# Weight units of half the size beside the row gathers of a two-block kernel

## The reference

```python
def peer(x, w_query, sub_keys, expert_down, expert_up):
    xt = x.reshape(T, D)
    qry = (xt @ w_query).reshape(T, H, 2, PEER_HALF_DIM)
    s = jnp.einsum('thpd,phnd->thpn', qry, sub_keys).astype(jnp.float32)
    ...
    gates = jax.nn.softmax(best_s, axis=-1).astype(x.dtype)
    ...
        u = expert_down[ib]
        act = jax.nn.gelu(jnp.einsum('td,thkd->thk', xb, u), approximate=False)
        vv = expert_up[ib]
        return jnp.einsum('thk,thkd->td', gb * act, vv)
```

## Time and profile before

| what | us |
|---|---|
| median of 3 runs | 3343.69 |
| lowest and highest of them | 3337.65, 3343.89 |
| the profiled execution | 3336.91 |
| its span in the trace | 3335.1 |
| PE busy in the span | 3110.8 (93%) |
| DMA: bytes moved, mean rate | 1206.86 MB, 362 GB/s |

### The profile page before, as it was taken

How to read it: one execution, slowest core, us unless ns; L and a number is a source line. 1 busy time by engine, 2 the same in 40 slices (tenths; PEclk the granted TensorE clock), 3 DMA queues, 4 the chain that set the end, 5 groups by cost and what they waited for, 6 DMA issues and landing times.

```text
span 3335.1 us, 24932 instructions
## 1 busy us (share of the span) xinstructions
PE 3110.8 (93%) x8525; PEld 1372.6 (41%) x8525; DVE 1087.6 (33%) x1830; ACT 570.1 (17%) x1356; POOL 641.3 (19%) x598
## 2 busy tenths in 40 slices
PE   8999998899999999998799989989799989999999
PEld 4444443444444444444244433434354533333344
DVE  1100014342334322335555544433432132222220
ACT  1110001111112110112224221221222111001010
POOL 1000002222224222223333332333300000000000
PEclk9999999999999999999999999999999989999999
DMA  9878887999989999999999999999967749999982
GB/s 351 305 273 294 307 299 292 414 370 360 397 343 396 421 417 407 402 411 405 420 408 419 418 419 419 419 419 417 416 220 267 258 194 422 422 422 422 422 310 76
DMA packets 266327, 1206.86 MB, mean 362 GB/s; under 512 B 14912, under 2 KB 17520, under 8 KB 162928
## 3 DMA queue, kind: packets, MB, share of 16 engines
q1 hardware_dynamic: 191872, 668.08, 52.0%
q0 software_dynamic: 74352, 537.48, 39.4%
HBM read 1203.41 MB, written 2.10 MB: 361 GB/s over the span
## 4 chain that ended last, share of the span: by engine, by line
PE 60%; DMA 30%; DVE 3%; issue 3%; ACT 1%; SPq 1%; DVEq 1%; POOL 0%; ACTq 0%; POOLq 0%
DMA W<-in_peer_expert_down,big 14%; PE bank L918 13%; PE bank L1469 11%; PE bank L987 8%; DMA W<-in_w_expert_up 8%; PE bank L1081 6%; PE bank L909 5%; PE bank L1576 4%; PE bank L1634 3%; DMA XS<-in_peer_expert_up,big 3%; DMA W<-in_w_in 3%; PE bank L1345 2%; DVE W L2517 1%; DMA W<-in_w_peer_query 1%; PE bank L1560 1%
## 5 line engine op out<-in xcount | busy, mean ns | idle before, releaser
L2517 DVE CUSTOM_DVE_ANT_0 W<-W,big 128x2048 f32<-128x2048 f32 x256 | 585.7, 2291 | 746.6 <-DMA W<-in_peer_expert_down,big 745.2
L1469 PE MATMUL bank<-XS,big 128*128 128x512 f32 x1040 | 497.1, 624 | 85.2 <-DMA XS<-in_peer_expert_up,big 45.0
L849 POOL DMA_INDIRECT W<-in_peer_expert_down,big x256 | 295.7, 1155 | 1027.0 <-issue 508.7
L1469 PEld LDWEIGHTS bank<-XS,big 128*128 128x128 f32 x1040 | 202.9, 200 | 356.8 <-issue 279.6
L918 PE MATMUL bank<-W,XT 128*128 128x512 f32 x704 | 308.2, 596 | 1.4 <-DMA W<-in_w_peer_query 1.4
L1469 PE MATMUL bank<-W,big 128*128 128x512 f32 x520 | 242.8, 611 | 41.4 <-ACT big L1913 32.6
L1469 PE MATMUL bank<-XT,big 128*128 128x512 f32 x488 | 225.6, 606 | 19.1 <-ACT big L1913 17.5
L1908 ACT ACTIVATE small<-small 128x1 f32<-128x1 f32 x256 | 51.7, 202 | 1111.6 <-DVE small L2517 1090.5
L1576 PE MATMUL bank<-W,XS 128*64 128x512 f32 x1024 | 225.1, 593 | 14.2 <-DMA W<-in_w_expert_up 11.5
L1081 PE MATMUL bank<-W,XT 128*128 128x512 f32 x480 | 217.6, 607 | 17.2 <-DMA W<-in_w_in 17.2
L856 POOL DMA_INDIRECT XS<-in_peer_expert_up,big x130 | 154.8, 1191 | 365.1 <-PE bank L1469 289.0
(11 more groups left out here) (374 smaller groups left out, 2563.6 us busy)
## 6 DMA issues: line engine op xcount, KB each, us to landing
W<-in_w_in SPq DMA_DIRECT2D x132, 2048.0 KB, 12.6
W<-in_w_expert_gate SPq DMA_DIRECT2D x68, 1024.0 KB, 15.0
W<-in_w_expert_up SPq DMA_DIRECT2D x68, 1024.0 KB, 17.0
W<-in_w_out SPq DMA_DIRECT2D x32, 2048.0 KB, 10.0
big<-in_w_expert_down SPq DMA_DIRECT2D x32, 2048.0 KB, 12.6
W<-in_w_ret_branch SPq DMA_DIRECT2D x16, 2048.0 KB, 8.2
W<-in_w_peer_query SPq DMA_DIRECT2D x16, 2048.0 KB, 12.7
W<-in_w_attn_branch SPq DMA_DIRECT2D x8, 2048.0 KB, 9.4
```

The costliest lines, as they stand in the source:

```text
L849: pool.indirect_dma_start(down_row(n), None, down_t, row).then_inc(down_in[n % DOWN_ROWS], 16)
L1469: mm = pe.matmul(bank[4 * (n // P) + c][:, :], DIAG[:, n % 4, :], up_row(n)[:, c * CH:(c + 1) * CH], start=n % P == 0, stop=n % P == P - 1)
L2517: dve.tensor_tensor_reduce(out=down_row(n), in0=down_row(n), in1=HN[n // P], scale=1.0, scalar=0.0, op0=ALU.mult, op1=ALU.add, accum_out=d ...
```

## The change

From `query 0 1 0` to the last `out2` unit of tile 0 a unit is half as large: half as many row blocks of the same columns (1.05 MB; of the wide matrices one row block by 2048 columns), 216 instead of 108. The four semaphores of the slots go on as four half slots of 2048 numbers over the memory of slots 0 and 1. A load waits for the last earlier unit that either used its semaphore or overlaps its memory. `PLACES` replaces the slot arithmetic, `depth` gives a unit's row blocks, and each unit function multiplies half as much per wait.

The tick table is adapted too: two halves are put where one unit was, or at half the spacing. Since the last half then falls later than the last whole unit fell, and the next step is counted from it, some steps move.

```diff
-    order += [("query", 0, c, half) for c in range(4) for half in range(2)]
-    order += [("in1", 1, g, j) for g in range(8) for j in range(2 if g == 1 else 4)]
+    order += [("query", 0, c, j) for c in range(4) for j in range(4 if c else 2)]
+    order += [("in1", 1, g, j) for g in range(8) for j in range(4 if g == 1 else 8)]
     for name in WIDE:
-        order += [(name, 1, j) for j in range(4 if name == "att" else 8)]
-    order += [("in2", 0, g, j) for g in range(5) for j in range(4)]
+        order += [(name, 1, j) for j in range(8 if name == "att" else 16)]
+    order += [("in2", 0, g, j) for g in range(5) for j in range(8)]
...
-TWO_SLOTS, FOUR_AGAIN = INDEX["query", 0, 1, 0], INDEX["in2", 1, 0, 0]
+HALVES, WHOLE_AGAIN = INDEX["query", 0, 1, 0], INDEX["in2", 1, 0, 0]
...
+    for i in range(len(ORDER)):
+        half = HALVES <= i < WHOLE_AGAIN
+        s = (i - HALVES if half else i - WHOLE_AGAIN if i >= WHOLE_AGAIN else i) % SLOTS
+        lo, hi = (2048 * s, 2048 * (s + 1)) if half else (UNIT * s, UNIT * (s + 1))
+        there = [j for j in range(i) if places[j][0] == s or places[j][1] < hi and lo < places[j][2]]
+        signals[s] += 16
+        places.append((s, lo, hi))
+        landed.append(signals[s])
+        earlier.append(there[-1] if there else None)
...
-    for i in range(4):
-        key = ("query", 0, 2 + i // 2, i % 2)
-        when[key] = int(i * 2.3)
+    for i in range(8):
+        key = ("query", 0, 2 + i // 4, i % 4)
+        when[key] = int(i * 1.15)
...
-        x = when["query", 0, c, 1]
+        x = when["query", 0, c, 3]
...
-        when[key] = at + i if i < 6 else int(at + 6 + (i - 6) * 1.25)
+        when[key] = at + i // 2 if i < 12 else int(at + 6 + (i - 12) * 0.625)
...
-            when[key] = int(at + i * 1.1)
+            when[key] = int(at + i * 0.55)
             put(pe, when[key], *key)
         x = when[units[-1]]
-        at = max(at + len(units) * 1.1, x + 2)
+        at = max(at + len(units) * 0.55, x + 2)
...
-        start, pace, hop = (134, 4, 1) if t == 0 else (261, 1, 0)
+        start, pace, hop = (134, 2, 1) if t == 0 else (261, 1, 0)
...
-                w = slot(i, D)
-                for c, k in [(c, k) for c in range(4) for k in range(2)] if first or last else [(c, k) for k in range(2) for c in range(4)]:
-                    if first and k == 0:
+                lhs = xt(j, 1) if at is None else P1[:, 1, at + j * P:at + (j + 1) * P]
+                for c in range(4):
+                    if first:
                         bank_free(name, c)
-                    b = 2 * j + k
-                    lhs = xt(b, 1) if at is None else P1[:, 1, at + b * P:at + (b + 1) * P]
-                    mm = pe.matmul(bank[4 + c][:, :], lhs, w[:, k, c * CH:(c + 1) * CH], start=first and k == 0, stop=last and k == 1)
+                    mm = pe.matmul(bank[4 + c][:, :], lhs, slot(i, D)[:, 0, c * CH:(c + 1) * CH], start=first, stop=last)
...
-                    for k in range(4):
+                    for k in range(2):
                         mm = pe.matmul(bank[c][:, :], lhs(k), slot(i, 1024)[:, k, c * CH:(c + 1) * CH],
-                                       start=first and k == 0, stop=last and k == 3)
+                                       start=first and k == 0, stop=last and k == 1)
```

More of the change, by code:

```diff
@@ L61 @@
 WIDE = ("gate_a", "gate_r", "att", "ret", "mix", "query")
-OUT2 = [[("out2", 0, g, j) for g in range(2) for j in (2, 3, 0, 1)],
+OUT2 = [[("out2", 0, g, j) for g in range(2) for j in (4, 5, 6, 7, 0, 1, 2, 3)],
         [("out2", 1, c, half) for half in (1, 0) for c in range(4)]]
@@ L65, with places_of_units @@
 INDEX = {key: i for i, key in enumerate(ORDER)}
-TWO_SLOTS, FOUR_AGAIN = INDEX["query", 0, 1, 0], INDEX["in2", 1, 0, 0]
+HALVES, WHOLE_AGAIN = INDEX["query", 0, 1, 0], INDEX["in2", 1, 0, 0]
 UG = INDEX["ple", 0]
[L68 to L74, removed]
+def places_of_units():
+    places, landed, earlier, signals = [], [], [], [0] * SLOTS
+    for i in range(len(ORDER)):
[7 more added lines that the diff above has]
+        earlier.append(there[-1] if there else None)
+    return places, landed, earlier
+PLACES, LANDED, EARLIER = places_of_units()
+SLOT = [place[0] for place in PLACES]
 def rows_of_up():
@@ L247, in steps_beside_picks @@
         for i, key in enumerate(OUT2[t]):
-            when[key] = start + (20 + i) * pace
+            when[key] = start + ((20 if t else 40) + i) * pace
             put(pe, when[key], *key)
-        x = {c: when["in2", 1, c, 1] if t else when["in2", 0, c // 2, 3] for c in range(10)}
+        x = {c: when["in2", 1, c, 1] if t else when["in2", 0, c // 2, 7] for c in range(10)}
         put(pe, start + 1, "forget", t)
@@ L316, in steps_beside_picks @@
         for c in range(4):
-            y = when["out2", 1, c, 0] if t else when["out2", 0, c // 2, 1]
+            y = when["out2", 1, c, 0] if t else when["out2", 0, c // 2, 3]
             put(dve, y + hop, "out2", t, c)
@@ L557, in slot, with depth @@
         def slot(i, n=CH):
-            return W[:, SLOT[i], :].rearrange("p (k n) -> p k n", n=n)
+            _, lo, hi = PLACES[i]
+            return W[:, :, :].rearrange("p s n -> p (s n)")[:, lo:hi].rearrange("p (k n) -> p k n", n=n)
+        def depth(key):
+            _, lo, hi = PLACES[INDEX[key]]
+            return (hi - lo) // columns(key)
         def columns(key):
@@ L680, in source @@
                 if kind == "in1":
[L681 to L691, removed]
+                    w, at = w_in, IN1[key[2]][0]
+                elif t == 1 and kind in WIDE:
+                    w, at = wide_from[kind], 0
+                elif kind == "query":
+                    w, at = w_q, CH * key[2]
+                elif t == 0 and kind == "in2":
+                    w, at = w2, col[CHUNK_E[2 * key[2]][0]]
+                elif t == 0 and kind == "out2":
+                    w, at = w_out2, 1024 * key[2]
+                else:
+                    w, at = None, 0
+                if w is not None:
+                    n, ks = columns(key), depth(key)
+                    return w.rearrange("(k p) n -> p k n", p=P)[:, ks * key[-1]:ks * key[-1] + ks, at:at + n]
                 if kind == "in":
@@ L701, in source @@
                     return rows(w_out, key[3], CH * key[2])
-                if kind == "query":
-                    return rows(w_q, key[3], CH * key[2])
                 if kind == "in2":
@@ L737, in _ @@
                 load(i)
-            sp.wait_ge(w_used, INDEX["ret", 1, 7] + 1)
+            sp.wait_ge(w_used, INDEX["ret", 1, 15] + 1)
             sp.dma_start(HN[1], A["ffn_norm"].to_broadcast([P, D])).then_inc(grow_loaded, 16)
-            for i in range(INDEX["query", 1, 0], INDEX["in2", 0, 0, 2]):
+            for i in range(INDEX["query", 1, 0], INDEX["in2", 0, 0, 4]):
                 load(i)
@@ L746, in _ @@
             sp.dma_start(GROW, A["final_norm"].unsqueeze(0).to_broadcast([P, D])).then_inc(grow_loaded, 16)
-            for i in range(INDEX["in2", 0, 0, 2], INDEX["in2", 1, 1, 0]):
+            for i in range(INDEX["in2", 0, 0, 4], INDEX["in2", 1, 1, 0]):
                 load(i)
@@ L853, in _ @@
                 elif b >= 3:
-                    pool.wait_ge(w_used, INDEX[("query", 1, 7) if b == 4 else ("query", 0, 3, 1)] + 1)
+                    pool.wait_ge(w_used, INDEX[("query", 1, 15) if b == 4 else ("query", 0, 3, 3)] + 1)
                 pool.sem_inc(gathers, 1)
@@ L916, in unit @@
                 pe.wait_ge(w_loaded[SLOT[i]], LANDED[i])
-                for k in range(8):
-                    mm = pe.matmul(out, lhs(k), slot(i)[:, k, :], start=first and k == 0, stop=last and k == 7)
+                ks = depth(key)
+                for k in range(ks):
+                    mm = pe.matmul(out, lhs(k), slot(i)[:, k, :], start=first and k == 0, stop=last and k == ks - 1)
                 mm.then_inc(w_used, 1)
@@ L980, in wide_unit @@
                         bank_free(name, c)
-                w = slot(i, D)
-                for c, k in [(c, k) for c in range(4) for k in range(2)] if first or last else [(c, k) for k in range(2) for c in range(4)]:
-                    if first and k == 0:
+                lhs = xt(j, 1) if at is None else P1[:, 1, at + j * P:at + (j + 1) * P]
+                for c in range(4):
+                    if first:
                         bank_free(name, c)
-                    b = 2 * j + k
-                    lhs = xt(b, 1) if at is None else P1[:, 1, at + b * P:at + (b + 1) * P]
-                    mm = pe.matmul(bank[4 + c][:, :], lhs, w[:, k, c * CH:(c + 1) * CH], start=first and k == 0, stop=last and k == 1)
-                    if last and k == 1 and c < 3:
+                    mm = pe.matmul(bank[4 + c][:, :], lhs, slot(i, D)[:, 0, c * CH:(c + 1) * CH], start=first, stop=last)
+                    if last and c < 3:
                         mm.then_inc(wide_chunk, 1)
@@ L1011, in turn1, with query_unit @@
```

(21 more changed lines are left out.)

19 lines of the change are left out of this document (9 added, 10 removed).

## The result

| what | us |
|---|---|
| before, median of 4 runs | 3340.86 (3337.65 to 3343.89) |
| changed, median of 4 runs | 3304.24 (3302.18 to 3304.39) |
| ratio, with its 95% interval | 0.9889 (0.9872 to 0.9906) |
| changed, profiled execution and span | 3304.09, 3302.1 |

The kernel became 36.6 us faster, 1.1%. The forecast was 3323, 20 us under the median shown then: the direction was right and the time lies inside the range, but the move was nearly twice the forecast.

The account below looks back on a forecast made before the run. By stretch, transfers, PE or neither bind the kernel. Halves -12 and -3, ticks -10 and longer waits +5 sum to -20 us: 3324 from a median of 3343.7, taken as 3323, range 3300 to 3350.

Parts of the forecast that it names:

- part 1: Halves in four half slots: refills go out sooner, giving weights more lead; -12 us in in1, -3 among the wide matrices.
- B: Stretch of in1, ticks 10 to 43, 364 us, bound by neither engine; 12 us back from lead, between 0 and 22.
- E: Stretch of picks alone, ticks 105 to 134, 153 us, bound by transfers; loses seven ticks at 5.1 us, -36.
- D: Stretch of the wide matrices, ticks 54 to 104, 492 us, bound by PE; lead -3 us, five more picks +17.
- F: Last stretch, 121 picks, 746 us, one unit in four picks, bound by transfers; change 0, within 3 us either way.
- Part 2: Moved ticks: picks leave the transfer-bound stretch of picks alone for one bound by PE; sum -11, taken as -10 us.
- A: First stretch, ticks 0 to 9, the last query units, 70 us, bound by transfers; grows two ticks, +10 us.
- Part 3: Later choose(4) costs 0, 5 us once if its tick is missed; gathers sharing with weights +5, between 0 and 20.
- The rival: Gathers starve: down rows land later and delay picks; decides if pick waits grow over 25 us; 3346 to 3375, 15%.
- The transfers bind all: Rival: in1's missing DMA share is the price of 4 KB runs, so halves give nothing; 3339 to 3343, 20%.
- More comes back: Rival: in1 recovers all 22 us, the wide matrices 8, gathers lose nothing; 3303 us, chance 15%.
- Slow transfers: Rival: 108 more, half-size transfers each leave a 3.3 us gap, a third on the path; 3460 us, chance 2%.

Follow-up runs that it names:

- Halves alone: Against the kernel before: halves in four half slots, both halves of a unit at the whole unit's old tick; 3316.14 us, ratio 0.9933.
- the ticks measure 13.3 alone: Against the kernel before: whole units in two slots, each at the tick of the changed kernel's second half; 3324.60 us, ratio 0.9954.

## Why the prediction was right in kind and short in size

The step that failed is a size in part 1: the 12 us for B, where 19 came back, and a cause left out beside it.

**What bounds the kernel, by stretch.** Right. The gain came where neither engine was full (B) and from moving picks between a stretch that the transfers bind (E) and one that PE binds (D). F, the longest, stayed within 3 us.

Of the signs it named, B (345 us at a share of 0.98), the waits for weights (3.7 us, below 8) and F (743 us against 740, cut alike) came as written. D took 503 us where 509 stood, and a pick in E 5.4 us (125 / 23) where 5.1 stood.

**Part 1, the lead.** The failing step is the value taken inside bounds that were right. For B the prediction had 0 and 22 us and took 12, with the reason that two engines can't both be full with so small a buffer. Halves alone took 19 us off B: with four half slots both engines were nearly full, at a clock of 0.99 and a DMA share of 0.97. The cap worked out from the DMA share, 342 us, was a good forecast of the 345. The reason against it rested on no row. The arithmetic of the lead (10.3 to 13.7 us against 13.7 to 17.2) described one of two causes; that PE starts on half a unit while the rest is still landing was left out, and it is worth 9 to 14 us of the changed kernel's gain, where the sooner refill is worth 6 to 11. D's term, 3 of 0 to 8, was right in size, 492 to 489, though it rested on no row either.

**Part 2, the ticks.** The method held. The places (12, 47, 56, 111, FIFTH at 116) are those of the code, and the prices of a tick, 3.4 us in D and 5.1 in E, came out at 3.4 and 5. The sum was taken as -10; the ticks measure 13.3 alone and some 13 on top of the halves (3316.1 to 3303.3, on two chips). The 3 that lack lie within the intervals. By stretch the forecast was +10 for A, -2 for B and C, +17 for D and -36 for E. From halves alone to the changed kernel the traces show +12, -10, +14 and -34, and +4 in F. The term that was too small is B and C, where the new places also took stops off the picks.

**Part 3, what waits longer.** The +5 for starved gathers was near in size as far as stops go: 4 us more of them before picks in A to D with halves alone. In the sum it has no place of its own beside B's 19 us, which are already net of it. Once the ticks moved, the waits before picks in A to D were 28.0 us against 28.5. The rival falls, since it needed 25 us more. The new waits and the issues of SP weren't tested alone; no row shows a cost of theirs. The 5 us named for a missed choose(4) were too much, some 1.4 us, but it isn't missed in the changed kernel: the indices come one step ahead, as worked out.

**The sum.** -12 - 3 - 10 + 5 = -20 against -19 - 3 - 13 + 0 = -35. Some 7 us of the difference are B, 5 the gathers, which were counted beside B instead of in it, and 3 the ticks. "The transfers bind all" falls with B. "More comes back", at 3303 and with a chance of 0.15, is nearest to what happened, but that it meets the time within 1 us is in part luck. It had 22 for B, 8 for D and 11 for the ticks, 41 in all from 3343.7; the runs gave 19, 3 and 13, and the median before came out at 3340.9. For B the upper bound was the better forecast, for D it was not.

**Slow transfers.** D moves 421 GB/s, with all its weights in transfers of 1.05 MB. The Trainium skill, DMA: Bandwidth & Descriptors, section Bandwidth, gives 341 GB/s for a transfer of 1 MB. No run here has one by itself, and D's, which overlap with others, run above that figure.

## What to carry to other kernels

When a buffer of fixed memory feeds an engine and both the engine and the DMA are near full, cut the unit before asking for more memory: four halves in place of two wholes freed 22 us here, in part because a slot is refilled sooner and in part, by the traces the larger one, because work starts on what has landed. When two kinds of work share a fixed order, price a step by what binds the stretch it stands in, and move it to where the other resource binds: a pick cost 5 us alone and 3.4 among the wide units. And when you forecast less than a bound that comes from rows, name the row that speaks for less: for B there was none, and 7 of the 16 us that the forecast missed lie there.

## What the runs showed that I had not expected

A stall of POOL of 9.9 us in the middle of a stretch that the transfers bind cost some 1.4 us there and left no mark on the total (3303.09 against 3303.42). The queue of gathers already issued, three down rows and up to four up rows of an estimated 2.5 us each (1.05 MB at 421 GB/s), is a buffer for the engine that issues them as much as for those that use them.
